# The head of a streaming encoder step: transposes by feature block over three token tiles, the norm gain behind them, and the first weight tile's products following block by block

## The reference

```
def _rmsnorm(x, g):
    x32 = x.astype(jnp.float32)
    y = x32 * lax.rsqrt(jnp.mean(x32 * x32, axis=-1, keepdims=True) + NORM_EPS)
    return (y * g.astype(jnp.float32)).astype(x.dtype)

h = _rmsnorm(x, g)                      # 1152 tokens x 2048 features
u = h @ w_in                            # 2048 -> 7688 columns
... four mixers on slices of u: chunk attention, mLSTM, short convolution, S5 with a GLU ...
x = x + y @ w_out                       # 2048 -> 2048
y_out = _rmsnorm(x, final_norm_g)
```

## Time and profile before

| | us |
|---|---|
| median of 3 runs | 2263.47 (2261.59 to 2264.64) |
| the profiled execution | 2262.94 |
| its span, first to last instruction | 2261.2 |
| TensorE busy | 2231.4 (99%) |
| VectorE busy | 798.8 (35%) |
| ScalarE busy | 474.6 (21%) |
| GpSimd busy | 430.6 (19%) |

### The profile page before, as it was taken

The page is one execution under the profiler, slowest core; times in us unless marked ns, Lnnn a source line. Parts: engine busy times, 40 slices in busy tenths (PEclk is TensorE's granted clock), DMA queues, the critical chain, the costliest instruction groups (busy, mean ns, idle before and its releaser), DMA issues.

```text
span 2261.2 us, 34823 instructions
## 1 busy us (share of the span) xinstructions
PE 2231.4 (99%) x14216; PEld 2076.9 (92%) x14216; DVE 798.8 (35%) x1342; ACT 474.6 (21%) x799; POOL 430.6 (19%) x259
## 2 busy tenths in 40 slices
PE   6999999999999999999999999999999999999998
PEld 6899999999999999999999999999998998888887
DVE  7231122222222111118665352222431364353633
ACT  6120122121222111111111111111101013343422
POOL 2132212222122221222222222222221120000000
PEclk9999999999999999999999999999999999999999
DMA  5131412324241444323333215333334547465552
GB/s 225 38 80 60 173 66 93 135 90 145 97 149 50 137 141 144 122 93 95 108 98 94 82 48 156 118 117 118 125 116 167 204 167 271 168 230 169 192 207 93
DMA packets 158525, 292.82 MB, mean 129 GB/s; under 512 B 28236, under 2 KB 97484, under 8 KB 155744
## 3 DMA queue, kind: packets, MB, share of 16 engines
q1 hardware_dynamic: 150368, 275.22, 36.4%
q10 hardware_dynamic: 8064, 16.25, 2.2%
HBM read 233.33 MB, written 76.92 MB: 137 GB/s over the span
## 4 chain that ended last, share of the span: by engine, by line
PE 97%; DVE 1%; DMA 1%; ACT 0%; SPq 0%; issue 0%; DVEq 0%; POOLq 0%
PE G L879 23%; PE G L881 22%; PE G L880 22%; PE X L1225 3%; PE G L1225 3%; PE G L1226 3%; PE X L1226 3%; PE G L1227 3%; PE X L1227 3%; PE X L980 1%; PE X L1202 1%; PE X L940 1%; PE X L971 1%; PE X L1094 1%; PE X L1004 1%; PE X L1069 1%
## 5 line engine op out<-in xcount | busy, mean ns | idle before, releaser
L879 PE MATMUL G<-hhi,whi 128*128 128x384 f32 x2880 | 981.7, 341 | 1.9 <-DVE hlo L1518 1.9
L881 PE MATMUL G<-hhi,wlo 128*128 128x384 f32 x2880 | 965.6, 335 | 0.0
L880 PE MATMUL G<-hlo,whi 128*128 128x384 f32 x2880 | 965.2, 335 | 0.0
L879 PEld LDWEIGHTS G<-hhi,whi 128*128 128x128 f32 x2880 | 541.9, 188 | 19.0 <-issue 12.7
L880 PEld LDWEIGHTS G<-hlo,whi 128*128 128x128 f32 x2880 | 542.1, 188 | 0.8
L881 PEld LDWEIGHTS G<-hhi,wlo 128*128 128x128 f32 x2880 | 541.6, 188 | 0.0
L859 POOL CAST whi<-wr 128x1024 fp32r<-128x1024 f32 x120 | 131.0, 1092 | 1384.6 <-PE G L881 1240.0
L861 POOL TENSOR_TENSOR wlo<-wr,whi 128x1024 fp32r<-128x1024 f32 x120 | 294.1, 2450 | 9.6
L1242 ACT ACTIVATE ev<-G 128x384 f32<-128x384 f32 x162 | 79.3, 489 | 720.6 <-PE G L881 720.5
L1993 DVE TENSOR_TENSOR olo<-orw,ohi 128x1024 fp32r<-128x1024 f32 x96 | 112.2, 1220 | 155.1 <-ACT ohi L1460 154.7
L1460 ACT ACTIVATE ohi<-orw 128x1024 fp32r<-128x1024 f32 x96 | 95.3, 1050 | 165.7 <-PE X L1227 61.5
(11 more groups left out here) (361 smaller groups left out, 1890.0 us busy)
## 6 DMA issues: line engine op xcount, KB each, us to landing
wr<-w_in_t SPq DMA_DIRECT2D x120, 512.0 KB, 5.5
orw<-w_out_t SPq DMA_DIRECT2D x96, 512.0 KB, 5.0
u_scratch<-ev SPq DMA_DIRECT2D x174, 192.0 KB, 1.9
xin<-x_all SPq DMA_DIRECT2D x9, 1024.0 KB, 5.0
yr<-y_scratch SPq DMA_DIRECT2D x12, 768.0 KB, 8.0
xo<-x_all SPq DMA_DIRECT2D x3, 3072.0 KB, 11.8
y_all<-fo SPq DMA_DIRECT2D x18, 512.0 KB, 2.7
kc<-k_cache SPq DMA_DIRECT2D x8, 1024.0 KB, 5.6
```

The source lines that it names most:

```text
L879: mm(G[:, j, 0:GC], whi[:, kh, k], hhi[:, kk, hs], start=(kk == 0), stop=False)
L880: mm(G[:, j, 0:GC], whi[:, kh, k], hlo[:, kk, hs], start=False, stop=False)
L881: last = mm(G[:, j, 0:GC], wlo[:, kh, k], hhi[:, kk, hs], start=False, stop=(kk == 15))
```

## The change

The head is written anew on all engines.

- The rows of a token tile are multiplied by the reciprocal root alone (`norm`, now a multiplication with one scalar per partition; for tile 2 in four pieces of four blocks). The gain is applied behind the transposes, where features are partitions and it is one scalar per partition and block, `gcol`, 128 by 16 numbers (8 KB in place of 1 MB): as the `scale` of ACT's copy into `hhi` and as the first factor in DVE's remainder into `hlo`.
- Transposes go by feature block: for block `k` of third `j`, three 128x128 transposes, one for each token tile of the third, fill 384 columns of one bank. `n` counts these 48 steps through the head (16 for each third). Five banks of `X` are used in turn. ACT and DVE work on 128x384 for each step.
- The product of a block follows its transposes at a distance of four steps (`X_AHEAD`): three transposes of step `n`, then three matmuls of step `n - 4`, and so on through all 48.
- All nine token tiles have a place of their own: tiles 0 to 2 in `xin`, 3 to 5 in the part of `hlo` and 6 to 8 in the part of `hhi` that belongs to the last third (`x_lo`, `x_hi`). No load waits for a slot. In those places a tile is not one run of 8 KB per partition but 16 runs of 512 bytes. Tiles 4 and 5 share a semaphore that is waited for when both are in, tiles 6, 7 and 8 likewise.
- For tiles 3 to 5 and 6 to 8, ACT squares them after its copies of blocks 2, 6 and 9 of the third before (`SQUARE_AT`), takes the root two copies later, and DVE normalizes after its remainder three blocks later. The unread output of the squares goes to `sqd`.
- SP issues tile 0, weight half 0, tiles 1 and 2, the gain, weight half 1, tiles 3 to 5, the gate weights, tiles 6 to 8.
- POOL splits both halves of weight tile 0 ahead of the gate weights; the second half waits until tile 2 is normalized (`xn_done` at 6).
- ACT takes one root of no use at the very start, ahead of the first square.

Everything behind the head's last product is as it was. The changed lines, without those that only rename:

```diff
+        xstack = ExitStack()
+        x_hi = sb(xstack, "x_hi", [128, KT, NT])
+        x_lo = sb(xstack, "x_lo", [128, KT, NT])
+        xstack.close()
+
...
-        xin = sb(st0, "xin", [128, 4, D])
-        gb = sb(st0, "gb", [128, D])
+        xin = sb(st0, "xin", [128, 3, KT, 128])
+        sqd = sb(st0, "sqd", [128, KT, 128])
+        gcol = sb(st0, "gcol", [128, KT])
...
+        def x_tile(t):
+            n = slice(2 * GC + 128 * (t % 3), 2 * GC + 128 * (t % 3) + 128)
+            return xin[:, t] if t < 3 else (x_lo if t < 6 else x_hi)[:, :, n]
+
+        def x_sem(t):
+            return (x_in[t], 16) if t < 4 else (x_in[4], 32) if t < 6 else (x_in[5], 48)
...
-            def load_x(t, s):
-
-                sp.wait_ge(xt_mm, 4 * t + 4)
-                sp.dma_start(xin[:, s], x_all[ds(t * 128, 128), :]).then_inc(x_in[s], 16)
-
-            load_x(0, 0)
-            sp.dma_start(gb[:, :], g_in).then_inc(g_loaded, 16)
-            for s in range(1, 4):
-                load_x(s, s)
+            def load_x(t):
+                sp.dma_start(x_tile(t), x_all[128 * t:128 * t + 128, :].rearrange("p (k n) -> p k n", k=KT)).then_inc(x_sem(t)[0], 16)
+
+            load_x(0)
             load_w(0, 0)
+            load_x(1)
+            load_x(2)
+            sp.dma_start(gcol[:, :], g_in).then_inc(g_loaded, 16)
             load_w(0, 1)
+            for t in range(3, 6):
+                load_x(t)
             sp.dma_start(gw[:, :, :], w_gate).then_inc(gate_w, 16)
-            for s in range(4):
-                load_x(4 + s, s)
-            load_x(8, 0)
+            for t in range(6, TT):
+                load_x(t)
...
+            def split(T):
+                for kh in range(2):
+                    pool.wait_ge(wraw[kh], 16 * T + 16)
+
+                    if kh == 0:
+                        pool.wait_ge(half0_mm, T + 1)
+                    else:
+                        pool.wait_ge(bank_full, 3 * T + 3)
+                    if isinstance(T, int) and kh == 1:
+                        pool.wait_ge(xn_done, 6)
+                    pool.sem_inc(w_turn, 1)
+                    g.tensor_copy(whi[:, kh], wr[:, kh]).then_inc(whi_done, 1)
+                    pool.wait_ge(whi_done, 2 * T + kh + 1)
+                    g.tensor_tensor(wlo[:, kh], wr[:, kh], whi[:, kh].bitcast(F), ALU.subtract).then_inc(w_split, 1)
+
+            split(0)
             pool.wait_ge(gate_w, 16)
             g.tensor_copy(gx[:, :, 0:8], gw[:, :, :]).then_inc(gate_w, 1)
             pool.wait_ge(gate_w, 17)
             g.tensor_tensor(gx[:, :, 8:16], gw[:, :, :], gx[:, :, 0:8].bitcast(F), ALU.subtract).then_inc(gate_w, 1)
+            with pool.Fori(1, NTILES) as T:
+                split(T)
...
-            def gemm(T, kh, j, first=False):
+            def product(kk, j):
+                kh, k = kk // 8, kk % 8
+                hs = slice(GC * j, GC * j + GC)
+                mm(G[:, j, 0:GC], whi[:, kh, k], hhi[:, kk, hs], start=(kk == 0), stop=False)
+                mm(G[:, j, 0:GC], whi[:, kh, k], hlo[:, kk, hs], start=False, stop=False)
+                return mm(G[:, j, 0:GC], wlo[:, kh, k], hhi[:, kk, hs], start=False, stop=(kk == 15))
+
+            def gemm(T, kh, j):
...
-            def xpose(t, s):
-                pe.wait_ge(xn_done, t + 1)
-                for qd in range(4):
-                    pe.wait_ge(h_done, 4 * t + qd + 1)
-                    for k in range(4):
-                        last = tr(X[:, qd, 128 * k:128 * k + 128],
-                                  xin[:, s, 512 * qd + 128 * k:512 * qd + 128 * k + 128], ident[:, :])
+            def xpose(n, i):
+                return tr(X[:, n % 5, 128 * i:128 * i + 128], x_tile(3 * (n // KT) + i)[:, n % KT], ident[:, :])
+
+            for i in range(3):
+                pe.wait_ge(xn_done, i + 1)
+                for n in range(X_AHEAD):
+                    last = xpose(n, i)
+                    if i == 2:
+                        last.then_inc(xt_mm, 1)
+            for n in range(X_AHEAD, 3 * KT + X_AHEAD):
+                if n < 3 * KT:
+                    pe.wait_ge(xn_done, n // 4 + 3 if n < KT else 3 * (n // KT) + 6)
+                    pe.wait_ge(h_done, n + 1)
+                    for i in range(3):
+                        last = xpose(n, i)
                     last.then_inc(xt_mm, 1)
-
-            for t in range(TT):
-                xpose(t, t % 4)
-                if t in (3, 4, 6, 7):
-                    gemm(0, t % 3, t // 3 - 1, first=True)
-            for kh in range(2):
-                gemm(0, kh, 2, first=True)
+                m = n - X_AHEAD
+                j, kk = m // KT, m % KT
+                if kk % 8 == 0:
+                    pe.wait_ge(w_split, kk // 8 + 3)
+                pe.wait_ge(h_done, m + 6)
+                last = product(kk, j)
+                if kk == KT - 1:
+                    last.then_inc(bank_full, 1)
+                elif j == 2 and kk == 7:
+                    last.then_inc(half0_mm, 1)
             pe.wait_ge(gate_w, 18)
             for j in range(3):
                 gs_ = slice(GC * j, GC * j + GC)
...
 
             def square(t):
-                act.wait_ge(x_in[t % 4], 16 * (t // 4) + 16)
-
-                fn(hlo[:, :, 128 * t:128 * t + 128], xin[:, t % 4].rearrange("p (k n) -> p k n", k=KT), ACT.Square,
-                   accum_out=stat[:, 0, t:t + 1]).then_inc(sq_done, 1)
+                act.wait_ge(*x_sem(t))
+                fn(sqd[:, :, :], x_tile(t), ACT.Square, accum_out=stat[:, 0, t:t + 1]).then_inc(sq_done, 1)
 
             def root(t):
                 act.wait_ge(ms_done, t + 1)
                 fn(stat[:, 2, t:t + 1], stat[:, 1, t:t + 1], ACT.Sqrt).then_inc(rms_done, 1)
 
-            def high(t):
-                for qd in range(4):
-                    act.wait_ge(xt_mm, 4 * t + qd + 17)
-                    fn(hhi[:, 4 * qd:4 * qd + 4, 128 * t:128 * t + 128], X[:, qd].rearrange("p (k n) -> p k n", k=4),
-                       ACT.Copy).then_inc(hhi_done, 1)
-
-            for t in range(2):
+            act.wait_ge(const_done, 7)
+            fn(stat[:, 2, 0:1], ident[:, 0:1], ACT.Sqrt)
+            for t in range(3):
                 square(t)
                 root(t)
-            for t in range(TT):
-                if t + 2 < TT:
-                    square(t + 2)
-                high(t)
-                if t + 2 < TT:
-                    root(t + 2)
+            act.wait_ge(g_loaded, 16)
+            for n in range(3 * KT):
+                act.wait_ge(xt_mm, n + 1)
+                j, k = n // KT, n % KT
+                fn(hhi[:, k, GC * j:GC * j + GC], X[:, n % 5, 0:GC], ACT.Copy, scale=gcol[:, k:k + 1]).then_inc(hhi_done, 1)
+                if j < 2 and k in SQUARE_AT:
+                    square(3 * j + 3 + SQUARE_AT.index(k))
+                if j < 2 and k - 2 in SQUARE_AT:
+                    root(3 * j + 3 + SQUARE_AT.index(k - 2))
             def evac_su(T):
                 for j in range(3):
                     act.wait_ge(bank_full, 3 * T + j + 4)
...
-                stt(xin[:, t % 4], xin[:, t % 4], stat[:, 3, t:t + 1], gb[:, :], MUL, MUL).then_inc(xn_done, 1)
-
-            def low(t):
-                for qd in range(4):
-                    dve.wait_ge(hhi_done, 4 * t + qd + 1)
-                    sl = (slice(None), slice(4 * qd, 4 * qd + 4), slice(128 * t, 128 * t + 128))
-                    tt(hlo[sl], X[:, qd].rearrange("p (k n) -> p k n", k=4), hhi[sl].bitcast(F), SUB).then_inc(h_done, 1)
-
-            for t in range(2):
+                for q in range(4) if t == 2 else (slice(0, KT),):
+                    ks = slice(4 * q, 4 * q + 4) if t == 2 else q
+                    x = x_tile(t)[:, ks]
+                    tsc(x, x, stat[:, 3, t:t + 1], None, MUL).then_inc(xn_done, 1)
+
+            for t in range(3):
                 mean(t)
                 rstd(t)
-                if t == 0:
-                    norm(0)
-            for t in range(TT):
-                if t + 1 < TT:
-                    norm(t + 1)
-                if t + 2 < TT:
-                    mean(t + 2)
-                low(t)
-                if t + 2 < TT:
-                    rstd(t + 2)
+                norm(t)
+            dve.wait_ge(g_loaded, 16)
+            for n in range(3 * KT):
+                dve.wait_ge(hhi_done, n + 1)
+                j, k = n // KT, n % KT
+                sl = (slice(None), k, slice(GC * j, GC * j + GC))
+                stt(hlo[sl], X[:, n % 5, 0:GC], gcol[:, k:k + 1], hhi[sl].bitcast(F), MUL, SUB).then_inc(h_done, 1)
+                if j < 2 and k - 1 in SQUARE_AT:
+                    mean(3 * j + 3 + SQUARE_AT.index(k - 1))
+                if j < 2 and k - 3 in SQUARE_AT:
+                    rstd(3 * j + 3 + SQUARE_AT.index(k - 3))
+                    norm(3 * j + 3 + SQUARE_AT.index(k - 3))
 
 
             g = Chain(dve, gt_dve)
...
+X_AHEAD = 4
+SQUARE_AT = (2, 6, 9)
...
```

(1 more changed line is left out.)

23 lines of the change are left out of this document (8 added, 15 removed).

## The result

| | before | after |
|---|---|---|
| median of 13 runs each, us | 2263.58 (2260.44 to 2265.48) | 2267.96 (2263.61 to 2269.34) |
| the profiled execution | 2262.94 | 2267.71 |
| its span | 2261.2 | 2266.0 |
| first gate matmul, the head's end | 71.05 | 67.33 |

The ratio is 1.0022, 95% interval 1.0014 to 1.0029: the changed kernel is 4.4 us slower. Forecast were 2258.2, a range of 2253 to 2265.5, and a chance of 0.09 for slower. The head did become shorter. What it gained, and more, was lost behind it, where the diff changes nothing.

What follows compares the result with a forecast made beforehand. TensorE was taken as busy nearly throughout, so only gaps or low clock could be won. 26.9 + 21.4 + 14.5 + 1.4 + 1.1 + 0.5 put the head's end at 65.8, not 71.05: 5.2 gained, median 2258.2, range 2253 to 2265.5.

Steps and rivals of the forecast that it cites:

- the sum's last: Behind the head: gate matmuls and everything after start at 65.8 and keep their length, so the 5.2 us gain stays.
- (c): Head's tile loads: runs of 512 bytes at half rate, 5 us a tile; end 73.0, time 2265.4; chance 0.07.
- (d): Head: TensorE's clock stays low, half its instructions being transposes; end at 90, time 2282; chance 0.03.
- First product: Start of the head: TensorE's first product at 17.2 us, where it was at 31.4.
- Step: Head: three transposes and three matmuls take 0.92 us at full clock, with 0.83 as the lower bound.
- the turn from three transposes to a product: Each head step with transposes: the first matmul behind them costs 0.09 us more.
- Low clock at the start: Start of the head: TensorE's clock low until about 22 us, three steps at 1.6, 2.2 us lost.
- a wait of 2.79: Head, product 7: TensorE waits 1.0 us because ACT's square of tile 4 needs tiles 4 and 5 in, at 23.8.
- rival (b)'s second half: Head: TensorE's clock falls in waits of 1.4 and 1.1, each fall costing 1.9 us; time 2262; rival's chance 0.18.
- hand-over waits: Head, where the second and third thirds begin: TensorE waits 1.4 and 1.1 us for normalized tiles.
- the new order's start: Start of the head: loads in the new order bring the first product at 17.2 us.
- normalization at 1.3 us: Head, VectorE: normalizing a tile by one scalar per partition takes 1.3 us, where it took 2.35 before.
- the place where ScalarE would stand: Head: ACT idle behind copy 6, from about 21 until tiles 4 and 5 are in at 23.8.

Runs made afterwards that it cites:

- e8: Changed kernel with 38 implied waits of the first stage left out, so later TensorE code stands where it stood before; 2263.82 us, ratio 0.9992.
- e2: Kernel before with 38 further, already met waits ahead of TensorE's first transpose; 2269.87 us, ratio 1.0024.
- e9: Kernel before with 38 met waits spread behind the attention loop, in its last pair; 2267.41 us, ratio 1.0014.
- e3: Changed kernel with a semaphore or a value of one for each token tile's load; 2266.40 us, ratio 1.0002.
- e5: Changed kernel with the output product starting on half of VectorE's remainders; 2265.18 us, ratio 1.0004.
- e4: Kernel before with the output product starting on half of VectorE's remainders; 2264.55 us, ratio 0.9998.
- e11: Kernel before with 100 further met waits behind the attention loop; 2267.55 us, ratio 1.0016.
- e6: As e5, with 38 implied waits for the remainder in the first stage left out; 2262.35 us, ratio 0.9991.
- e12: As e10, with 100 further met waits behind the attention loop; 2262.70 us, ratio 0.9995.
- e10: Changed kernel with the 38 waits left out and own semaphores for tiles 4 to 8; 2257.34 us, ratio 0.9974.

## Why the prediction was wrong

**The step that failed** is the sum's last: "Gate matmuls and all behind them start from there and keep their length." They did not. The head ended 3.73 us earlier and the last matmul started 4.74 later, so 8.5 us were added behind it. e8, e2 and e9 show that 38 instructions more in TensorE's stream are a cause: placed back (e8), the time is less than the changed kernel's by 4.1 us by the medians and by 6.8 by the two ratios, and the old head with them (e2) is 5.4 slower. At the two turns they cost 2.2 in the changed kernel (0.8 to 1.3 each in after, e2, e3 and e5; nothing in the kernels with the loop where it was, or a block further on). The other 2 us between the two traces lie at the load of `mqkv` and at the output product; that fetches beside the loads cost them is likely, and not shown for each. The remaining 4.2 us are lost in e8 as well, with no fetch moved: there the chain on VectorE, not TensorE, set when the output product could start, and TensorE waited 3.6 us and ran at the low clock for 3.4 behind it. So the step fails twice, by the place of the code and by a wait that takes up a gain. The prediction had a term for neither: it priced VectorE's and ScalarE's work in the head and did not ask what TensorE's added waits move, nor what the last matmuls wait for. It had no rival of this kind either: (c) and (d), its slower ones, both lay in the head and neither happened.

**The measure was taken from one execution.** The earlier trace rows show the low clock at 61 to 65 us before, and I took the head's end of 71.05 as given. Two later kernels with the old head word for word show the same stretch at full clock. Before, and e4:

```profile
61.00:65.00 4.00, 3.94 (x14) 3.94 (x15) 0.00 (x1) 0.33 (x1) 0.00 (x0) 0.57 0.50 98
```

```profile
61.00:65.00 4.00, 4.00 (x25) 4.00 (x24) 0.00 (x0) 0.00 (x0) 0.00 (x0) 1.00 0.50 98
```

The old head ended at 71.05, 70.94 (e11), 68.87 (e4) and 68.69 (e9); in the last two the clock had been low earlier, from 22 us on, while TensorE waited for tiles anyway. (With 38 waits ahead of it, in e2, it ended at 67.87.) The new one ended at 67.3 to 67.5 in the four traces that have it (after, e5, e6, e8). The gain is therefore 1.4 to 3.7, some 2.5 in the mean, and not 5.2; against a mean of the old head at 69.9 the forecast of 65.8 would itself have been a gain of 4.1. Of it e8 keeps 1.8 at the end by its ratio (by the interval between 3.8 faster and 0.2 slower).

**The terms of the head.** First product 17.86 instead of 17.2: copy and remainder of a first block took 0.58 and 0.62, more than in a run. Step 0.85 instead of 0.92: the turn from three transposes to a product costs 0.02, not the 0.09 seen behind sixteen; over the 36 steps behind product 7 that is 2.5 us in favour. Low clock at the start until 19.2 in this execution, not 22: only the first step took longer, 1.47, so 0.6 us was lost and not 2.2 (in e3 it lasted until 22.2, and three steps took 1.6, 1.6 and 1.4). One short wait at product 6, 0.50, cancels part of this. Tile 5 in at 25.06 instead of 23.8, and a wait of 2.79 where I had 1.0; weight half 1 landed at 14.0 instead of 13.3, and tiles 3 to 5 at 17.63, 21.25 and 25.06, 3.7 us each and not 3.5. Behind it the clock fell for 3.4 us (29.4 to 32.9), half of which is lost: rival (b)'s second half, which I had tied to waits of 1.4 and 1.1. The hand-over waits were 0.79 and 1.18 for 1.4 and 1.1, and 1.21 more came ahead of two products of the second third. In sum 67.33 for 65.8.
The page "TensorE: Matmul & The Clock Gate" of the Trainium skill, section "Part 4: PE-mode transpose", had stood behind rival (d). The changed kernel, where half of TensorE's instructions up to 52 us are transposes, ran at a granted clock of 1.00 from 34 to 46: the row decides against the rival. It does not test the page's rule by itself, since matmuls of 384 columns fill 0.52 of each step's 0.85 us.

**What was right:** the new order's start (within 0.7 us), normalization at 1.3 us, the place where ScalarE would stand, the hand-over waits (0.6 off and 0.1 off).

**What stays open:** why one fetch of 1 us delays a transfer by up to 2.3. Issuing is slower beside it (the sixteen issues, 8.5 for 7.4 us), but the three loads of `mqkv` that TensorE waits for were issued in 1.8 us in e9 and 1.9 before, and the third landed 7.1 us after its issue instead of 5.7. e11 and e12 have slow loads without a fetch inside. Why the loop stays in at one place and not 38 instructions further on isn't shown either: its length in blocks is the same. And how long VectorE's chain before the output product takes also depends on how it meets GpSimd's splits, which I did not vary by itself; e8 against e10 suggests that this decides whether a gain in the head survives.

## What to carry to other kernels

When an edit adds or removes instructions on an engine whose program has loops, compare the count of its instruction fetches and the idle time put down to "issue" at each loop's start, before looking at anything else; a version with the same shift and no other edit (e2, e9) separates the shift from the change. A gain at the start of a program is worth only what the next wait on a transfer or another engine lets through, so follow the distance between the two traces to the end and price each place where it changes. And take a stretch's length from several executions if the clock falls in it.

## What the runs showed of the hardware

- A loop of some 1680 TensorE instructions (6.6 blocks of 256) turned without a fetch when 2862 or 3118 instructions stood ahead of it, and with fetches and 0.8 to 1.3 us lost at each turn when 2900 did.
- A 512 KB store landed in 2.8 us in twelve traces without an instruction fetch beside it, and in 4.8 and 4.9 in the two with one. Sixteen issues of SP took 7.4 us in the same twelve and 8.5 in the two. For the loads of `mqkv` and the convolution a fetch inside went with 0.3 to 2.3 us more than before, but loads without one reached 8.0 and 7.9 us too.
- 218 instructions that only wait, for a semaphore long reached, held TensorE until 27.45 us, at most 0.13 each. Spread between matmuls, 38 of them cost nothing (gate matmuls at 67.5 in e5 and e6, at 67.3 in after and e8).
- The old head's clock fell at 61 us in two of four executions with the same code, and in the other two it was low from 22 us on instead; the head's end differed by 2.1 us.
- A VectorE operation of 1024 or 1152 columns that takes 1.3 us took 3.4 or 3.5 beside a GpSimd split.
